# Decode reads through a padded query, fed products moved, scatter by halves, and ScalarE issuing the decode rows' store

## What is computed

```
layer 0: x @ w_in -> q,k,v,gates and z,xbc,dt
         4 GLA heads:  S_t = diag(exp(g_t)) S_{t-1} + k_t^T v_t ;  o_t = q_t S_t   (state 128 x 256)
         16 SSD heads in 2 groups: the same with a scalar decay (state 128 x 64 a head)
         RMS norm of each head, gate, output product, residual, layer norm
layer 1: the same with 8 HGRN2 heads (state 128 x 128)
each layer ends with a mixture of 16 experts (top 2 of one group), residual, layer norm
```

## Time and profile before

| | |
|---|---|
| median of 3 runs (lowest, highest) | 1032.12 us (1032.03, 1035.11) |
| the profiled execution, its time | 1031.38 us |
| its span, first to last instruction | 1029.7 us |
| TensorE, matmuls | 977.8 us busy, 95% |
| TensorE, weight loads | 631.6 us, 61% |
| VectorE, ScalarE, GpSimd | 38%, 27%, 10% |
| mean granted TensorE clock | 0.986 |
| GLA heads / SSD groups | about 38 to 160 us / 160 to 237 us |
| experts, layer 0 / layer 1 | about 314 to 552 us / 775 to 1013 us |
| HGRN2 heads | about 605 to 733 us |

### The profile page before, as it was taken

How to read it: one execution, slowest core, us unless ns; L and a number is a source line. 1 busy time by engine, 2 the same in 40 slices (tenths; PEclk the granted TensorE clock), 3 DMA queues, 4 the chain that set the end, 5 groups by cost and what they waited for, 6 DMA issues and landing times.

```text
span 1029.7 us, 12780 instructions
## 1 busy us (share of the span) xinstructions
PE 977.8 (95%) x5031; PEld 631.6 (61%) x5031; DVE 388.3 (38%) x936; ACT 277.0 (27%) x591; POOL 107.9 (10%) x177
## 2 busy tenths in 40 slices
PE   8999999899989999999997998999989999999995
PEld 6777777688866454545444876777866354545443
DVE  2467786773025021212113335665235021212114
ACT  4534434223023110000002166777123100100002
POOL 2322224161000000000000001112200000000000
PEclk9999999899998999999999999999999999999999
DMA  9933536947751999999999343332692999999991
GB/s 386 356 156 123 210 138 229 394 178 297 285 194 33 424 411 424 421 420 422 422 422 427 145 164 121 138 130 87 254 374 89 423 413 423 420 422 421 422 378 44
DMA packets 39183, 299.65 MB, mean 291 GB/s; under 512 B 5000, under 2 KB 6536, under 8 KB 8648
## 3 DMA queue, kind: packets, MB, share of 16 engines
q1 hardware_dynamic: 33696, 268.52, 64.1%
q0 software_dynamic: 4928, 29.72, 7.8%
q10 hardware_dynamic: 496, 0.53, 0.1%
HBM read 283.32 MB, written 15.53 MB: 290 GB/s over the span
## 4 chain that ended last, share of the span: by engine, by line
PE 76%; ACT 8%; DVE 7%; DMA 6%; issue 2%; POOL 1%; ACTq 0%; DVEq 0%; POOLq 0%
PE bank L1182 20%; PE bank L1206 10%; PE bank L827 9%; PE bank L1076 6%; PE bank L1218 5%; PE bank L1167 5%; PE bank L1330 4%; PE bank L1096 2%; PE bank L1343 2%; DMA ring<-in_w_up 2%; ACT ring L1515 2%; PE bank L1110 1%; PE bank L1104 1%; DMA spread<-v_rows 1%; DMA W<-in_conv_cols 1%
## 5 line engine op out<-in xcount | busy, mean ns | idle before, releaser
L1182 PE MATMUL bank<-ring,A 128*64 128x512 f32 x880 | 223.0, 592 | 2.3 <-issue 1.7
L827 PE MATMUL bank<-xT,ring 128*128 128x264 f32 x704 | 165.0, 390 | 2.7 <-ACT A L1428 1.4
L827 PEld LDWEIGHTS bank<-xT,ring 128*128 128x128 f32 x704 | 132.0, 191 | 32.7 <-issue 9.3
L1182 PEld LDWEIGHTS bank<-ring,A 128*64 128x64 f32 x880 | 73.8, 137 | 123.9 <-issue 123.9
L1206 PE MATMUL bank<-ring,W 128*64 128x512 f32 x448 | 113.4, 595 | 0.9 <-ACT W L1658 0.9
L2223 DVE TENSOR_TENSOR W<-W,bank 128x512 f32<-128x512 f32 x16 | 11.0, 688 | 203.6 <-PE bank L1182 203.6
L1343 PE MATMUL bank<-xT,ring 128*128 128x264 f32 x320 | 80.0, 395 | 0.0
L1206 PEld LDWEIGHTS bank<-ring,W 128*64 128x64 f32 x448 | 34.9, 137 | 60.9 <-issue 59.8
L754 POOL TENSOR_SCALAR xT<-xT,vecs 128x264 f32<-128x264 f32 x4 | 5.6, 1396 | 604.3 <-DVE xT L2077 604.3
L1343 PEld LDWEIGHTS bank<-xT,ring 128*128 128x128 f32 x320 | 58.4, 192 | 11.0 <-issue 1.8
L1218 PE MATMUL bank<-W,A 128*128 128x264 f32 x256 | 63.5, 392 | 1.7 <-issue 1.7
(11 more groups left out here) (310 smaller groups left out, 1180.5 us busy)
## 6 DMA issues: line engine op xcount, KB each, us to landing
ring<-in_w_gate SPq DMA_DIRECT2D x56, 1024.0 KB, 13.2
ring<-in_w_down SPq DMA_DIRECT2D x56, 1024.0 KB, 13.4
ring<-in_w_up SPq DMA_DIRECT2D x54, 1024.0 KB, 16.2
ring<-in_w_ab SPq DMA_DIRECT2D x10, 2048.0 KB, 8.2
ring<-in_w_c SPq DMA_DIRECT2D x8, 2048.0 KB, 13.7
A<-in_w_up SPq DMA_DIRECT2D x10, 1024.0 KB, 13.9
ring<-in_w_oab SPq DMA_DIRECT2D x4, 2048.0 KB, 9.2
A<-in_w_gate SPq DMA_DIRECT2D x8, 1024.0 KB, 12.8
```

The lines of the kernel that those rows point to most:

```text
L827: mm = pe.matmul(ab_bank(m)[:, 0:T], slot(AB_IN0 + m // 4, 8)[:, c, (m % 4) * P:(m % 4 + 1) * P], xT[:, c, :], start=(c == 0), stop=(c == ...
L1182: mm = pe.matmul(bank[i][64 * j:64 * j + 64, :], xg[:, 2 * (pair % 2) + j, c, :], slot(n0 + 6 * pair + 2 * i + j, 8)[:, c, :], start=(c == ...
```

## The change

The query is written into a zeroed area of 8 windows of 32 columns, token 4i+q into column i of its window. The reads of the second four tokens accumulate onto those of the first, and row 32q+i of one tile holds the read of token 4i+q. Squares, sums, roots, scaling and READ are half as wide. The turn is a plain transpose into bank 6 (bank 2 or 4 for the last head of a layer), from which VectorE takes the 8 columns. The wait for placed reads moves from `scores` to `turn_v` two heads later; `turn_out` gets a wait for the next head's `dec_v`. SSD the same, into bank 7. Two products of `C_FEED` move from behind `turn_out` to ahead of it. `scatter` waits for its own half of Y. ScalarE issues the store of `dec_v`; in layer 1 it copies v of head 0 ahead of the exps of head 1. The area of the padded query overlaps `s_eg`, so `spread_eg(0)` is issued after the GLA stage, behind `spread_x(0)`.

```diff
-C_FEED = (2, 2, 1, 2, 2, 1, 2, 2, 0, 2, 2, 2)
+C_FEED = (2, 4, 1, 0, 2, 1, 2, 2, 0, 2, 2, 2)
...
+        def query_columns(h):
+            at = 5632 + 256 * (h % 2)
+            return W[:, at:at + 258].rearrange("p (i x) -> p i x", x=129)[:, :, 0:P:32]
+        def padded_query(h, b):
+            at = 5632 + 256 * (h % 2) + 32 * b
+            return W[:, at:at + 32]
...
-            return bank[4][:, 256:256 + J * NB] if layer else bank[2][:, 400:400 + J * NB]
+            return bank[{3: 2, 11: 4}.get(n, 6)][:, 256:256 + J * P]
...
(gpsimd)
+            st.add(pool.memset(W[:, 5632:6144], 0.0))
...
-                pool.wait_ge(sem("heads_kv_copied"), 3 * n + 2)
-                pool.dma_start(v_rows[layer][h], dec_v[:, 0:dv]).then_inc(sem("heads_rows_stored"), 16)
                 pool.wait_ge(sem("heads_rows_stored"), 16 * (n + 1))
...
-            spread_eg(0)
             pool.wait_ge(sem("heads_out_ready"), 3)
...
             spread_x(0)
+            spread_eg(0)
...
(before layer 1's heads)
-            st.run(pool.memset(SC_BLOCKS, 0.0))
+            st.add(pool.memset(SC_BLOCKS, 0.0))
+            st.add(pool.memset(W[:, 5632:6144], 0.0))
+            st.settle()
...
(tensor, turn_v)
+                    if h >= 3:
+                        pe.wait_ge(sem("heads_reads_placed"), n - 2)
...
(tensor, scores)
-                    if h >= 2:
-                        pe.wait_ge(sem("heads_reads_placed"), n - 1)
...
(tensor, the reads)
-                            mm = pe.matmul(bank[3][32 * q:32 * q + 32, i * dv:(i + 1) * dv],
-                                           QS[:, h % 2, b:b + 1].to_broadcast([P, 32]), decode_state(layer, h, b),
-                                           start=True, stop=True)
+                            mm = pe.matmul(bank[3][32 * q:32 * q + 32, 0:dv],
+                                           padded_query(h, b), decode_state(layer, h, b),
+                                           start=(i == 0), stop=(i == 1))
...
(tensor, turn_out)
-                    for i in range(NB // 4):
-                        for j in range(J):
-                            mm = pe.matmul(read_turned(layer, J)[:, j * NB + 4 * i:j * NB + 4 * i + 4],
-                                           READ[:, i * dv + j * P:i * dv + (j + 1) * P], every32, start=True, stop=True)
-                    mm.then_inc(sem("heads_reads_turned"), 1)
+                    pe.wait_ge(sem("heads_kv_copied"), 3 * min(n + 2, H0 + nh - 1) + 2)
+                    for j in range(J):
+                        tr = pe.transpose(read_turned(H0 + h, J)[:, j * P:(j + 1) * P], READ[:, j * P:(j + 1) * P], ident[:, :])
+                    tr.then_inc(sem("heads_reads_turned"), 1)
...
(tensor, SSD)
-                        mm = pe.matmul(bank[5 + 2 * i][32 * q:32 * q + 32, :], CT[:, NP + b:NP + b + 1].to_broadcast([P, 32]),
-                                       ssd_state(g, b).rearrange("p h v -> p (h v)"), start=True, stop=True)
-                    mm.then_inc(sem("ssd_reads_ready"), 1)
+                        mm = pe.matmul(bank[5][32 * q:32 * q + 32, :], s_cz[:, 32 * b:32 * b + 32],
+                                       ssd_state(g, b).rearrange("p h v -> p (h v)"), start=(i == 0), stop=(i == 1))
+                    if i == 1:
+                        mm.then_inc(sem("ssd_reads_ready"), 1)
...
                 reads(0)
+                reads(1)
                 feed(4)
                 pe.wait_ge(sem("ssd_prompt_state"), g + 1)
-                reads(1)
-                for i in range(2):
-                    pe.wait_ge(sem("ssd_reads_copied"), 2 * g + i + 1)
-                    for j in range(4):
-                        mm = pe.matmul(bank[4][:, 256 + j * NB + 4 * i:260 + j * NB + 4 * i],
-                                       s_read[:, i, j * P:(j + 1) * P], every32, start=True, stop=True)
-                mm.then_inc(sem("ssd_state_used"), 1)
+                pe.wait_ge(sem("ssd_reads_copied"), g + 1)
+                for j in range(4):
+                    tr = pe.transpose(bank[7][:, j * P:(j + 1) * P], s_read[:, j * P:(j + 1) * P], ident[:, :])
+                tr.then_inc(sem("ssd_state_used"), 1)
...
             out_part(0, gla_half)
+            pe.wait_ge(sem("ssd_outputs_read"), 3)
             out_part(1, gla_half)
...
(tensor, scatter)
-                    for i in range(2):
-                        pe.wait_ge(sem(f"y_copied{i}"), p + 2)
+                    pe.wait_ge(sem(f"y_copied{half}"), p + 2)
...
(scalar, copy_v, after the copy of dec_v)
+                    act.wait_ge(sem("heads_kv_copied"), 3 * (H0 + h) + 2)
+                    act.dma_start(v_rows[layer][h], dec_v[:, 0:dv]).then_inc(sem("heads_rows_stored"), 16)
...
+                if layer == 1:
+                    copy_v(0)
                 exps(layer, 1)
                 st.run(act.activation(decx[:, 0:nh, :], (gkg[:, 0:4, NP:T] if layer == 0 else A[:, 8:16, NP:T]), ACT.Exp))
-                copy_v(0)
+                if layer == 0:
+                    copy_v(0)
...
(scalar, SSD: one copy of 128x512 in place of two; vector, SSD: s_cz cleared once, its 8 columns written in each group, L2046 reads bank 7 with a stride)
...
(vector, scaled)
-                    for i in range(2):
-                        st.add(dve.tensor_scalar(READ[:, i * dv:(i + 1) * dv], bank[3][:, i * dv:(i + 1) * dv],
-                                                 hms[:, h % 2, 2 + i:3 + i], None, ALU.mult))
+                    st.add(dve.tensor_scalar(READ[:, 0:dv], bank[3][:, 0:dv], hms[:, h % 2, 2:3], None, ALU.mult))
...
(vector, place_reads)
-                    dve.tensor_copy(oa(h)[:, :, NP:T], read_turned(layer, J).rearrange("p (j b) -> p j b", j=J)).then_inc(
-                        sem("heads_reads_placed"), 1)
+                    for j in range(J):
+                        put = dve.tensor_copy(oa(h)[:, j, NP:T].rearrange("p (i q) -> p q i", i=2),
+                                              read_turned(H0 + h, J)[:, j * P:(j + 1) * P].rearrange("p (q r) -> p q r", q=4)[:, :, 0:2])
+                    put.then_inc(sem("heads_reads_placed"), 1)
```

More of the change, by code:

```diff
@@ L447, in trunk_program @@
         hms = sb("hms", [P, 2, 4])
-        QS = area(9232, 2, NB)
-        READ = area(9248, 512)
+        READ = area(9248, 256)
+        def query_columns(h):
[4 more added lines that the diff above has]
+            return W[:, at:at + 32]
         def decode_state(layer, h, b):
@@ L500, in score_bank, with read_turned @@
             return bank[4 if layer else 2]
-        def read_turned(layer, J):
-            return bank[4][:, 256:256 + J * NB] if layer else bank[2][:, 400:400 + J * NB]
+        def read_turned(n, J):
+            return bank[{3: 2, 11: 4}.get(n, 6)][:, 256:256 + J * P]
         def x_spread(b):
@@ L526, in trunk_program @@
         XB_LATE = area(7168, 2, 512)
-        s_read = area(8320, 2, 512)
+        s_read = area(8320, 512)
+        s_cz = W[:, 8832:9088]
+        s_cz_columns = W[:, 8832:9090].rearrange("p (i x) -> p i x", x=129)[:, :, 0:P:32]
         s_sq = area(9344, 4, T)
@@ L1489, in squares @@
                     act.wait_ge(sem("heads_reads_ready"), n + 1)
-                    act.activation(READ[:, 0:2 * dv], bank[3][:, 0:2 * dv], ACT.Square, scale=dv ** -0.5).then_inc(
+                    act.activation(READ[:, 0:dv], bank[3][:, 0:dv], ACT.Square, scale=dv ** -0.5).then_inc(
                         sem("heads_squared"), 1)
@@ L1497, in roots @@
                     act.wait_ge(sem("heads_sums"), n + 1)
-                    st.run(act.activation(hms[:, h % 2, :], hms[:, h % 2, :], ACT.Ln, bias=eps_col[:, :]))
-                    act.activation(hms[:, h % 2, :], hms[:, h % 2, :], ACT.Exp, scale=-0.5).then_inc(sem("heads_roots"), 1)
+                    st.run(act.activation(hms[:, h % 2, 0:3], hms[:, h % 2, 0:3], ACT.Ln, bias=eps_col[:, :]))
+                    act.activation(hms[:, h % 2, 0:3], hms[:, h % 2, 0:3], ACT.Exp, scale=-0.5).then_inc(sem("heads_roots"), 1)
                 def place_out(h):
@@ L1586, in _ @@
                 act.sem_inc(sem("ssd_state0"), 1)
-                for i in range(2):
-                    act.wait_ge(sem("ssd_reads_ready"), 2 * g + i + 1)
-                    act.copy(s_read[:, i, :], bank[5 + 2 * i][:, :]).then_inc(sem("ssd_reads_copied"), 1)
-                    if i == 0:
-                        take_ab(m0 + 5)
+                act.wait_ge(sem("ssd_reads_ready"), g + 1)
+                act.copy(s_read[:, :], bank[5][:, :]).then_inc(sem("ssd_reads_copied"), 1)
+                take_ab(m0 + 5)
                 act.wait_ge(sem("ssd_outputs_read"), 2 * g + 2)
@@ L1840, in queries @@
                 def queries(h):
-                    st.run(dve.tensor_scalar(QS[:, h % 2, :], qa(h)[:, NP:T], scale, None, ALU.mult))
+                    st.run(dve.tensor_scalar(query_columns(h), qa(h)[:, NP:T].rearrange("p (i q) -> p i q", i=2), scale, None, ALU.mult))
```

(8 more changed lines are left out.)

8 lines of the change are left out of this document (4 added, 4 removed).

## The result

The changed kernel takes 1018.4 us (median of 4 runs, 1016.49 to 1023.78), the kernel before 1032.07 us (4 runs, 1029.75 to 1035.11): ratio 0.9857, 95% interval 0.9819 to 0.9895. So 13.7 us are gained in the medians. The profiled execution of the changed kernel happens to be its longest run: 1023.78 us (span 1021.7 us), 7.6 us less than the profiled execution of before (1031.38 us). So the two profiles explain less than the 13.7 us of the medians.

The account below looks back on a forecast made before the run. TensorE, busy 95% of the span, was taken as the bound, along with gaps before it. Seven terms summed to 17.6 us, giving 1013.8 us, 1014.5 off the median, forecast as 1014 us; range 1009.5 to 1021.5 us.

Parts of the forecast that it names:

- The forecast case: Whole kernel: faster, 1014 us, within 1010 to 1018 us; chance 0.72.
- Turns of layer 0, 1.7 us: GLA heads 0 to 2: two plain transposes replace L930's 8 instructions, saving 0.57 us each; head 3 counts nothing.
- SSD, 2.7 us: SSD groups 0 and 1: four transposes replace 16 instructions in the turn of the reads, saving 1.34 us each.
- First GLA head, 1.0 us: Layer 0, first head: an earlier store of decode rows shifts the chain and shrinks TensorE's 1.40 us gap.
- Scatter by halves, 1.7 us: Last pair of each layer: TensorE's 0.84 us wait for VectorE's copy of Y goes, twice.
- rival B: Expert stages: weight DMA sets the end and earlier gains are waited away; 1030 us, or 1022 at half effect; chance 0.06.
- First HGRN2 head, 3.6 us: Layer 1, first head: early row copies and ScalarE's store bring the first turn 3.6 us earlier; bounds 1.5 and 4.5.
- Steady heads, 5.6 us: Layer 1, between turns: period falls from 14.41 to 13.3 us, 1.1 us in each of five heads.
- Last turns, 1.3 us: Layer 1: the two last turns save 0.35 us each plus 0.27 us of a scaling, turn 7 itself 0.35 us.
- A (ScalarE): Heads: ScalarE's store issue and wait for its own copy make it the bound; 1020.4 us, chance 0.14.
- C (the turn waits for the store): Layer-1 heads: turn_out waits for the decode rows' store to land, making the kernel slower, 1036 us; chance 0.03.
- D: Chain not shortened: steady-head gain lost to exposed latency, GpSimd's decays meet VectorE elsewhere for 4.1 us; 1024 us, chance 0.05.

Follow-up runs that it names:

- hold: Changed kernel with SyncE holding the output-weight loads (w_oab) until the x rows of SSD group 1 are spread; 1014.0 us, ratio 0.9799.
- b_halves: Kernel before with only the scatter's wait changed, each half waiting for its own copy of Y; 1033.75 us, ratio 0.9998.
- repeat: The changed kernel run and profiled once more, unchanged; 1020.61 us, ratio 0.986 against the kernel before.
- x_pe: Changed kernel with ten further identity transposes on TensorE in each layer-1 head; 1026.46 us, ratio 0.9896.
- x_act: Changed kernel with two further squares of the reads on ScalarE in each layer-1 head; 1020.15 us, ratio 0.9839.
- u_store: Changed kernel with GpSimd again issuing the store of a head's decode rows; 1022.26 us, ratio 0.9871.
- b_swap: Kernel before with only VectorE's scores of SSD group 1 put ahead of its first four decode updates; 1030.87 us, ratio 0.9963.
- u_copyv: Changed kernel with layer 1's first-head row copies again behind the exps and the exp of the decays; 1023.59 us, ratio 0.9897.
- u_feed: Changed kernel with the fed products of a layer-1 head back in their old places; 1024.02 us, ratio 0.9881.

## Why the prediction was right, and where it wasn't

The forecast case, faster with a time inside the range, came true: 1018.4 us in 1009.5 to 1021.5. But 1014 us was too low, and the terms were less even than the sum. That the range was met is in part luck: ahead of layer 1 terms of 6.3 us gave nothing, while the heads of layer 1 gave 12.3 us where 10.5 us were forecast.

- **Turns of layer 0, 1.7 us: right.** Heads 1 and 2 give 56.82 - 55.57 = 1.25 us together, 0.6 each; head 3, costed at nothing, gives 0.03. Head 0 lies in the first stretch and can't be read by itself.
- **SSD, 2.7 us: the instructions right, the sum wrong.** The failing step is "both groups show the pattern" with nothing named that would be late next. Each group's work got 1.1 to 1.5 us shorter, but in group 1 TensorE then waited 4.9 us for VectorE, it for the x rows, and these for a DMA busy with the output weights. The stage took 75.6 to 76.7 us, against 75.03 and 76.74 us with the old code: nothing gained. Two views of before would have told. TensorE already waited 3.2 us for VectorE at the same place in group 0, and the x rows' spread already ended a wait of VectorE of 1.5 us in group 1.

```profile
PE bank L1033 <- DVEq L2022: 3.2, 1, 3.2
```

Hold shows that the loads of the output weights make the x rows late. Why TensorE lost nothing by it in before, and 3.2 us in b_halves with the same code there, is not shown.

- **First GLA head, 1.0 us: wrong.** I assumed that the rows would land earlier and that "the whole chain shifts". The spread was issued at 42.89 us instead of 45.83 (44.52 us in the repeat), but VectorE's first update started at 56.14 us (55.14 us) instead of 54.89. And a shift would have moved the meeting of L1834 with GpSimd's decay along with it, since that decay starts only when the update is over. Turn 0 came at 81.3 to 84.1 us in ten profiles of kernels with the new code and the old place of the decay, and at 80.9 to 81.8 us in the three with the old code. Moving the decay took the gap away.
- The rule cited there (the Trainium skill, SBUF — State Buffer, section "Who interferes with whom") says that two such instructions contend and that the one issued later is fully blocked. The contention is borne out: 4.54 us in company, 0.43 us alone. The order is not: by the rows VectorE's instruction starts first, at 61.11 us, and GpSimd's multiplies at 61.27 us take their usual 4.10 us.
- **Scatter by halves, 1.7 us: gap right, gain wrong.** Both gaps went; b_halves shows 0.9998 (0.9964 to 1.0031) for the whole, so no gain that can be told from none. In its profile the clock fell in the norm behind the one, and half of the other was waited for weights. The latter is rival B at small scale.
- **First HGRN2 head, 3.6 us: right** (29.24 - 25.63 = 3.6), but the split was not: 2.3 us from the early copies, none from the issuing engine.
- **Steady heads, 5.6 us: mechanism right, size low.** The working gave 13.2 us for TensorE and 13.3 us for the chain, about equal, and took the larger. Measured: 13.0 us, TensorE bound (x_pe), and the chain about 0.1 us shorter (x_act: 13.18 us with 0.31 us added, so 12.9 us without). Both were sized too long, the chain by 0.4 us. Five periods gave 7.1 us.
- **Last turns, 1.3 us: right**, 1.56 us.
- **Rivals.** A (ScalarE) is out, but narrowly: of 0.31 us added on ScalarE 0.20 us shows (x_act). Its own issue, 0.27 us, costs nothing: without it the turns are 13.11 us apart (u_store). C (the turn waits for the store) is out: no such wait. D's steady heads didn't come, and the meeting of decay and VectorE was the old one, which stayed.
- The Trainium skill, DMA: Bandwidth & Descriptors, section "Issuing engines are not separate DMA queues", says that another issuing engine saves only the time of the issue. That agrees with u_store: there the first spread is issued at 46.41 us and VectorE's update starts at 55.36 us, beside 42.89 and 56.14 us in the changed kernel, 44.52 and 55.14 us in its repeat.

## What to carry to other kernels

When TensorE gets faster ahead of a transfer, ask for each engine in the next stage which of its waits already ends on a DMA, even a wait of 1.5 us off the path. That is where the gain can be lost. And compare stages over more than one profile of the kernel before: here its own showed no loss in the stage, and b_halves, with the same code there, did. A small store in a chain (store, wait, spread) wants the bulk loads beside it held back until it is through: one wait on SyncE's queue took 6.5 us out of a stage in which the change itself gained nothing. And a gap of under 1 us taken out is not a gain until the stretch behind it has been read for the clock.

## What the runs showed of the hardware

- A 16 KB store landed in 1.8 us with the DMA moving 9 GB/s meanwhile (hold). Behind two loads of 2 MB it took longer, and longest where it followed them soonest: 7.9 us when issued 7.6 us after them (changed kernel, 359 GB/s meanwhile), 7.1 us at 10.3 us (repeat, 306 GB/s), 3.6 us at 13.1 us (before, 244 GB/s), 5.5 us at 14.2 us (b_halves, 143 GB/s). Only the last is out of order. The Trainium skill, DMA: Bandwidth & Descriptors, section "Anatomy of one DMA — SWDGE (gpsimd) path", gives a fixed cost of about 2 us for a transfer on this path; the case of hold agrees, the others are longer by up to 6 us.
- The granted clock in the norm of layer 0 (L1110, L1121) stayed at 1.00 in both profiled kernels with the old scatter (before, b_swap) and fell to 0.57 or less in some stretch of 2 us in all twelve profiles with the scatter by halves. Eleven of these have the rest of the change too; in b_halves the only difference of code is the scatter's wait, which takes out 0.84 us of idle time some 10 us earlier. The rows don't say why. In several kernels (u_store, u_copyv, u_feed, hold) it stayed low for longer, and the stretch took 60.9 to 62.6 us instead of 58.3. It may be part of the spread between runs; with one profile of most kernels that is not shown.
